# Visiting the two token halves to and fro in the plain projection products of a hybrid encoder step

## What is computed

```python
h = rmsnorm(x, g1)
z = h @ w_in                       # queries, keys, values, gates
mix = concat(window_attention(z), mlstm(z))
x = x + mix @ w_out
u = rmsnorm(x, g2) @ w_up          # 1024 -> 4096
x = x + square(relu(u)) @ w_down   # 4096 -> 1024
```

## Time and profile before

| | |
|---|---|
| median of 3 runs | 1319.53 us |
| the profiled execution | 1319.09 us |
| its span, first to last instruction | 1317.3 us |
| mean granted TensorE clock | 0.997 of full |
| matmuls | 9971, of them 6096 at line 1714 |
| TensorE busy | 1297.3 us (98%) |

### The profile page before, as it was taken

The page is one execution under the profiler, slowest core; times in us unless marked ns, Lnnn a source line. Parts: engine busy times, 40 slices in busy tenths (PEclk is TensorE's granted clock), DMA queues, the critical chain, the costliest instruction groups (busy, mean ns, idle before and its releaser), DMA issues.

```text
span 1317.3 us, 24640 instructions
## 1 busy us (share of the span) xinstructions
PE 1297.3 (98%) x9971; PEld 1268.5 (96%) x9971; DVE 899.5 (68%) x1494; ACT 611.0 (46%) x1134; POOL 62.6 (5%) x43
## 2 busy tenths in 40 slices
PE   7999999999999999999999999999999999999998
PEld 6999899999999999999999998999999999999997
DVE  7776787798486475586666768878965846846734
ACT  6324335488256155165242333456852732832833
POOL 0000001000000000000610000000000000000032
PEclk9999999999999999999999999999999999999999
DMA  8222220223232232222252222202332322322312
GB/s 222 80 71 66 63 65 33 81 70 123 65 96 98 66 94 96 91 68 96 86 120 71 65 65 65 65 33 81 97 97 65 97 97 65 113 78 73 120 65 72
DMA packets 115630, 109.74 MB, mean 83 GB/s; under 512 B 18830, under 2 KB 109398, under 8 KB 115542
## 3 DMA queue, kind: packets, MB, share of 16 engines
q1 hardware_dynamic: 110256, 104.54, 26.3%
q10 hardware_dynamic: 5286, 3.97, 1.0%
HBM read 104.69 MB, written 3.81 MB: 82 GB/s over the span
## 4 chain that ended last, share of the span: by engine, by line
PE 89%; DVE 6%; ACT 3%; issue 1%; DMA 0%; SPq 0%; ACTq 0%; DVEq 0%
PE psum L1714 56%; PE psum L2029 8%; PE psum L2031 8%; PE psum L2030 8%; PE psum L1767 1%; PE psum L1856 1%; PE psum L1945 1%; PE psum L1937 1%; PE psum L1910 1%; PE psum L1926 1%; PE psum L1954 1%; ACT w_hi L545 1%; PE psum L1887 1%; PE psum L1883 1%; PE psum L1874 0%
## 5 line engine op out<-in xcount | busy, mean ns | idle before, releaser
L1714 PE MATMUL psum<-hid_h,w_hi 128*128 128x288 f32 x1232 | 266.4, 297 | 0.0
L1714 PE MATMUL psum<-hid_l,w_hi 128*128 128x288 f32 x1232 | 263.7, 295 | 0.0
L1714 PE MATMUL psum<-hid_h,w_lo 128*128 128x288 f32 x1232 | 263.7, 295 | 0.0
L1714 PEld LDWEIGHTS psum<-hid_h,w_hi 128*128 128x128 f32 x1232 | 197.4, 188 | 1.1 <-issue 0.3
L1714 PEld LDWEIGHTS psum<-hid_h,w_lo 128*128 128x128 f32 x1232 | 197.4, 188 | 0.0
L1714 PEld LDWEIGHTS psum<-hid_l,w_hi 128*128 128x128 f32 x1232 | 197.4, 188 | 0.0
L1714 PE MATMUL psum<-xh,w_hi 128*128 128x288 f32 x800 | 178.5, 304 | 3.3 <-ACT x L590 2.3
L1599 DVE TENSOR_TENSOR tmp<-psum,rms 128x576 f32<-128x576 f32 x63 | 47.7, 757 | 186.0 <-PE psum L1714 185.9
L1714 PE MATMUL psum<-xh,w_lo 128*128 128x288 f32 x800 | 172.1, 296 | 0.0
L1714 PE MATMUL psum<-xl,w_hi 128*128 128x288 f32 x800 | 171.8, 296 | 0.0
L803 ACT ACTIVATE w_hi<-stage 128x1024 fp32r<-128x1024 f32 x64 | 67.7, 1058 | 219.0 <-PE psum L1714 218.2
(11 more groups left out here) (328 smaller groups left out, 2560.4 us busy)
## 6 DMA issues: line engine op xcount, KB each, us to landing
stage<-in_w_up SPq DMA_DIRECT2D x32, 1024.0 KB, 5.6
stage<-in_w_down SPq DMA_DIRECT2D x32, 1024.0 KB, 5.1
stage<-in_w_in SPq DMA_DIRECT2D x18, 1024.0 KB, 5.2
stage<-in_w_in SPq DMA_DIRECT2D x16, 256.0 KB, 4.5
stage<-in_w_out SPq DMA_DIRECT2D x8, 512.0 KB, 6.3
stage<-in_w_out SPq DMA_DIRECT2D x4, 1024.0 KB, 5.0
z<-in_x_prompt SPq DMA_DIRECT2D x4, 512.0 KB, 5.5
out<-z SPq DMA_DIRECT2D x3, 512.0 KB, 2.7
```

The costliest lines, as they stand in the source:

```text
L1714: ins = M(acc[t % 2][:, a, :], lhs(w), mov[:, k, a * HALF:(a + 1) * HALF], start=first and n == 0, stop=last and n == 2)
```

## The change

In `products` alone, the order in which the two halves are visited depends on the block `k` and on the number `n` of the product within it:

```diff
@@ -1710,7 +1710,7 @@
 
                 ins = None
                 for n, (w, mov) in enumerate(((w_hi, hi_mov), (w_hi, lo_mov), (w_lo, hi_mov))):
-                    for a in range(2):
+                    for a in ((0, 1) if (k + n) % 2 == 0 else (1, 0)):
                         ins = M(acc[t % 2][:, a, :], lhs(w), mov[:, k, a * HALF:(a + 1) * HALF],
                                 start=first and n == 0, stop=last and n == 2)
                 return ins
```

## The result

| | before | after |
|---|---|---|
| median | 1319.47 us (4 runs) | 1327.38 us (4 runs) |
| ratio, 95% interval | | 1.0061 [1.0049, 1.0072] |
| span of the profiled execution | 1317.3 us | 1325.8 us |

The prediction was 1313.7 us, range 1303.5 to 1323.0, with 0.24 on slower. The measured time lies above the range, on the side that was not forecast.

A forecast was written before the change was run, and what follows sets the result against it. TensorE's matmul stream at line 1714 was taken as the bound. 4500 matmuls gaining 7.2 us and 800 losing 1.4 us gave net -5.8 us, so 1313.7 us, range 1303.5 to 1323.

The forecast's parts named there:

- What bounds the kernel: TensorE's stream, above all line 1714 with 6096 matmuls, sets the time; TensorE busy 1297.3 of 1317.3 us.
- Two rhythms, not one number: At line 1714 matmuls start 130.0 ns apart in calm stretches, 133.3 ns in stalled ones.
- End of a tile: VectorE waits for the last matmul of both halves and reads both banks together, so the exchange costs nothing.
- The same bank twice in a row: At line 1714 each bank is now written twice in a row; claimed to cost nothing by itself.
- The order of what is read: At line 1714, reading halves 0 1 1 0 gives 131.7 ns per matmul, net -5.8 us.
- The calm is lost and nothing is gained: Rival: the 800 calm matmuls behind `sum_squares` go to 133.3 ns, +2.7 us or up to 1 more; chance 0.20.
- the calm groups: First groups' down tiles behind `sum_squares`, at 130.0 ns before; forecast to lose 800 x 1.7 = 1.4 us.
- More stalls: Rival: at line 1714 both changes of half cost 8 ns, 135.5 ns mean, +14.3 us, 1333.8 us; chance 0.07.
- The order does not matter: Rival: both rhythms at line 1714 stay where they are, 1319.5 us; chance 0.19.
- the 122.5 ns: The skill formula's gap for 288 columns, cited as a rule against; by it the change sums to zero.
- the 135.5 ns case: A stall of 8 ns twice as often at line 1714, 1333.8 us; chance 0.07, left out of the range.

The follow-up runs named there:

- e2: Kernel before with halves still read 0 1 0 1 but banks written 0 1 1 0 as in the change: 1319.30 us (1.0001).
- e1: Kernel before with halves read 0 1 1 0 as in the change but banks still written 0 1 0 1: 1327.33 us (1.0067).
- e6: Kernel before with halves read 0 1 0 1 0 1 in even blocks and 1 0 1 0 1 0 in odd ones: 1315.06 us (0.9969).
- e7: Kernel before with halves read 0 1, 1 0, 0 1 in every block: 1310.32 us (0.9932).
- e5: Kernel before with 64 instead of 128 bytes ahead of the split weights: 1316.41 us (0.9978).
- e10: Kernel before with every buffer moved up by 64 bytes, distances between operands kept: 1319.26 us (1.0000).
- e3: Kernel before without the 128 bytes ahead of the split weights: 1319.93 us (1.0008).
- e13: Kernel before with 384 instead of 128 bytes ahead of the split weights: 1319.31 us (1.0001).
- e14: Changed kernel with 384 instead of 128 bytes ahead of the split weights: 1327.40 us (1.0061 to the kernel before).
- e11: Kernel before with halves read 0 1, 1 0, 0 1 in every block and 64 bytes ahead of the weights: 1321.68 us (1.0018).
- e4: Changed kernel without the 128 bytes ahead of the split weights: 1325.51 us (1.0052 to the kernel before).

## Why the prediction was wrong, point by point

**What bounds the kernel** was right: 8.3 of the 8.5 us of added span are distances at line 1714, and no other wait shows in it.

**Two rhythms, not one number** was right, and it was what made the question answerable; the runs show not two but at least five settled rates, 130.0, 131.7, 132.2, 133.3 and 134.3 ns.

**End of a tile: nothing.** Right; matmuls elsewhere start as far apart as before, 478.8 us in sum against 478.6.

**The same bank twice in a row: nothing.** Right, and shown apart by e2: 1319.30 us.

**The order of what is read: 131.7 ns, -5.8 us.** This is the step that failed. That this term is the one that counts was right (e1), but its size and sign were not: the rate was 134.3. By the prediction's own sum, 4500 x 1.0 = 4.5 us and 800 x 4.3 = 3.4 us give +7.9, which is the measured difference of the medians; that it fits so well is luck in part. The counts were off: 1992 matmuls, not some 800, stand in short stretches, and 3336, not 4500, in the long ones outside the first groups. The short ones, which the sum left alone, lost 1.7 us. I built the rate of 0 1 1 0 as a value between the rates of 0 alone, 1 alone and 0 1, and with the idea that a sequence picks one of the rates already seen. The runs refute the mean: e6 settles at 131.7 and e7 mostly at 130.0, the change at 134.3, though all three read each half equally often. The second idea is false, since 134.3 is the settled rate of no stretch of these products before. Why 0 1 1 0 has this rate stays open. The row that was nearest in kind, sums that change their offset after every third matmul, 133.3 ns, I used for a rival only; it would have given 1322.2 us, still short by 5.

**Rivals.** "The calm is lost and nothing is gained" had the right place and sign, and its price, 2.7 us, is part of what happened (the calm groups lost 3.3). "More stalls" had the right side at nearly twice the price, but not by its mechanism: it wanted the 8 ns stall twice as often, two of four distances at about 140, and the trace has two longer distances, 145 and 153, once in 20, and the rest between 126 and 137, with matmuls of up to 313 ns where 302 was the longest. I gave it 0.07 because no view showed a settled stretch above 133.3. That a rate had not been seen said little, because the trace of before held only a handful of sequences. "The order does not matter" falls with e1. The Trainium skill's formula in "TensorE: Matmul & The Clock Gate" ("Back-to-back issue gap") has no term for addresses. The section gives it as the gap of an isolated matmul, and lists 81 and 131 ns for a stream of load and matmul pairs at 128 and 512 columns, so the 122.5 ns was the wrong figure of it to hold against a stream. No run here has those two widths; at 288 columns and full clock these runs spread over 4.3 ns by the order and the place of what is read alone. The Trainium skill's page "SBUF — State Buffer" gives weight loads a second, independent read port ("A bandwidth-pool intuition that's wrong (but worth ruling out)"). e5 against e10, and e3's last tile, show that the rate depends on where the weights lie relative to the moving operand, so the two do affect each other somewhere. Where, no run here shows: whether it is the reads themselves, a clash in the array or in the issue stayed untested. Nor is it shown why 256 bytes is the period, or what makes a stretch fall into one rhythm rather than another.

**Range.** It was built from settled rates of the old sequences. Since a new sequence has a rate that none of these bounds, its upper end should have held at least the 135.5 ns case, 1333.8 us, at more than 0.07.

## What to carry to other kernels

When a stream of matmuls fills the time, measure its distance from start to start over a hundred matmuls in each stretch; a spread of 1 to 3% at the same shape and clock is worth an experiment with the order of reads and with the weights' offset against the activations, a few multiples of 64 bytes, together and not one by one. Do not forecast the rate of a new sequence from those of its parts: here three orders of the same reads gave -0.7%, -0.3% and +0.6%, and the best turned to +0.2% when 128 bytes became 64. Any edit that moves a buffer may shift such rates too, so a small change of time should be checked against them before it is put down to the edit's purpose.

## What the runs showed of the hardware that was not expected

- 128x128 by 288 fp32r matmuls with a weight load each run at 130.0 to 134.3 ns from start to start at full clock. The distances repeat with a fixed period (2 or 4 before, 20 in the change) and the rate is constant over hundreds of matmuls.
- The rate follows the sequence of read addresses relative to the weights (e5, e10), and not the order of the PSUM banks (e2). Another 256 bytes change nothing (e13, e14), and 128 bytes less exchange the rates of the two halves when each is read alone (e3's last tile).
- The same sequence can have two settled rates: 0 1 runs at 130.0 in the first groups, behind `sum_squares`, and at 133.3 in the other groups; e7's order at 131.7 or 130.0, with 64 bytes (e11) at 132.2 or 133.3; the change's order with no offset (e4) at 133.3 or 134.3. In e2 a stretch of 264 matmuls behind the first `sum_squares` was calm, which was stalled in the profile of before, a difference of 0.9 us by itself. This may be what spreads the runs of the kernel before over some 2 us (1318.1 to 1320.3), but that was not tested.
